# Four reorderings in a three-block transformer kernel: an output feature begun early, two copies moved, conversions cut in halves, a subtraction moved

## The reference

```
# block 1, sparse attention ("sparse stage")
score = sum_h relu(qi_h . ki) * w_h ; keep the 128 best keys of each token
p = softmax(q . k over the kept keys);  o = p @ c;  x += o @ a_w_out
# block 2, retention: 4 heads of 256, values of 512
s = (rotary(q) rotary(k)^T) * decay ; ret = s @ v
x += (rms_norm(ret) * silu(g)) @ b_w_out
# block 3, gated stage: three branches, each with a gate
y_a = (gelu u * spatial gating of v) @ w_a_out ; y_b = conv branch @ w_b_out
z = q k^T / 8 ; a = exp(log_sigmoid(z) + sum over later keys of log_sigmoid(-z))
y_c = (a @ v) @ w_c_out
x += (g0*y_a + g1*y_b + g2*y_c) @ w_out_2
```

## Time and profile before

| | us |
|---|---|
| median of three runs | 2094.62 |
| the profiled execution's own time | 2094.45 |
| its span, first to last instruction | 2092.7 |
| TensorE busy | 2077.5 (99%) |
| VectorE busy | 1461.1 (70%) |
| GpSimd busy | 1236.8 (59%) |
| ScalarE busy | 1145.1 (55%) |

### The profile page before, as it was taken

The page is one execution under the profiler, slowest core; times in us unless marked ns, Lnnn a source line. Parts: engine busy times, 40 slices in busy tenths (PEclk is TensorE's granted clock), DMA queues, the critical chain, the costliest instruction groups (busy, mean ns, idle before and its releaser), DMA issues.

```text
span 2092.7 us, 31674 instructions
## 1 busy us (share of the span) xinstructions
PE 2077.5 (99%) x11883; PEld 1819.7 (87%) x11883; DVE 1461.1 (70%) x2383; ACT 1145.1 (55%) x1892; POOL 1236.8 (59%) x763
## 2 busy tenths in 40 slices
PE   9999999999999999999999999999999999999999
PEld 7867889889899989988899898888887888899998
DVE  7973786767588777777776675997577325785773
ACT  6564654654554546456645544446777435645642
POOL 3514665874687778546658744655432554848843
PEclk9999999999999999999999999999999999999999
DMA  4203323333323232332333334322222242333232
GB/s 169 71 12 94 91 93 101 109 102 104 114 71 96 77 110 86 95 99 87 95 93 113 106 89 173 104 82 77 71 71 70 92 135 89 102 101 104 89 109 94
DMA packets 57687, 200.82 MB, mean 96 GB/s; under 512 B 6400, under 2 KB 7168, under 8 KB 57280
## 3 DMA queue, kind: packets, MB, share of 16 engines
q1 hardware_dynamic: 56816, 197.46, 29.9%
q10 hardware_dynamic: 720, 1.34, 0.2%
HBM read 194.32 MB, written 4.19 MB: 95 GB/s over the span
## 4 chain that ended last, share of the span: by engine, by line
PE 59%; DVE 1%; ACT 1%; issue 0%; ACTq 0%; DVEq 0%
PE ps L431 13%; PE ps L432 13%; PE ps L433 13%; PE ps L734 5%; PE ps L736 5%; PE ps L735 5%; PE ps L459 1%; PE ps L460 1%; PE ps L461 1%; PE ps L3005 1%; PE ps L2990 0%; PE ps L3017 0%; DVE ACC L632 0%; PE ps L2992 0%; PE ps L3014 0%
## 5 line engine op out<-in xcount | busy, mean ns | idle before, releaser
L409 POOL TENSOR_TENSOR WL<-WS,WH 128x1024 fp32r<-128x1024 f32 (+1 forms) x240 | 567.5, 2368 | 525.3 <-ACT WH L399 524.8
L431 PE MATMUL ps<-H,WH 128*128 128x512 f32 (+2 forms) x1264 | 492.9, 390 | 1.2 <-DVE H L639 0.7
L432 PE MATMUL ps<-H,WH 128*128 128x512 f32 (+2 forms) x1264 | 490.7, 388 | 0.0
L433 PE MATMUL ps<-H,WL 128*128 128x512 f32 (+2 forms) x1264 | 490.5, 388 | 0.0
L1246 POOL TENSOR_TENSOR WL<-WS,WH 128x512 fp32r<-128x512 f32 x232 | 312.3, 1359 | 226.5 <-ACT WH L857 224.6
L399 ACT ACTIVATE WH<-WS 128x1024 fp32r<-128x1024 f32 (+2 forms) x242 | 248.7, 1029 | 135.5 <-PE ps L433 66.6
L431 PEld LDWEIGHTS ps<-H,WH 128*128 128x128 f32 (+1 forms) x1264 | 237.0, 188 | 51.0 <-issue 2.7
L433 PEld LDWEIGHTS ps<-H,WL 128*128 128x128 f32 (+1 forms) x1264 | 236.9, 187 | 49.4
L432 PEld LDWEIGHTS ps<-H,WH 128*128 128x128 f32 (+1 forms) x1264 | 237.1, 188 | 46.3
L431 PE MATMUL ps<-G,WH 128*128 128x512 f32 x496 | 193.7, 391 | 2.2 <-DVE G L2724 1.4
L432 PE MATMUL ps<-G,WH 128*128 128x512 f32 x496 | 193.1, 389 | 0.0
(11 more groups left out here) (410 smaller groups left out, 4950.5 us busy)
## 6 DMA issues: line engine op xcount, KB each, us to landing
WS<-in_w SPq DMA_DIRECT2D x337, 512.0 KB, 3.5
WS<-in_w SPq DMA_DIRECT2D x24, 384.0 KB, 3.1
xs<-X SPq DMA_DIRECT2D x1, 2048.0 KB, 6.3
X<-xs SPq DMA_DIRECT2D x8, 256.0 KB, 3.7
out<-X SPq DMA_DIRECT2D x8, 256.0 KB, 2.0
X<-in_sg SPq DMA_DIRECT2D x1, 1344.0 KB, 5.6
X<-in_x ACTq DMA_DIRECT2D x4, 256.0 KB, 6.0
X<-in_x SPq DMA_DIRECT2D x4, 256.0 KB, 5.5
```

The source lines that it names most:

```text
L409: e.tensor_tensor(lo, raw, hi.bitcast(F), ALU.subtract).then_inc(*P.sig("w_lo", i))
L431: e.matmul(out, lh, rh, start=start, stop=False)
L432: e.matmul(out, lh, rl, start=False, stop=False)
L433: return e.matmul(out, ll, rh, start=False, stop=stop)
```

## The change

Four edits, none of which adds or removes arithmetic apart from the cut of three conversions.

1. Sparse stage: feature 2 is begun too (`D_OUT` has a third entry, 39, so its first half comes after the steps and ahead of TensorE's wait); features 3 to 7 remain whole. ScalarE makes unit 2's high part at its step 36.
2. Retention: in head 0, `u2` of the first gate pair goes ahead of two `decayed` copies and a form. In heads 0 to 2, `p5` of the k pair goes ahead of `y_high(h, 0)` and gets a wait for the row of head h.
3. Retention: the low part of `("bout", h, 0)`, h = 0 to 2, is made in two halves of 128x512, and TensorE waits for the first before z = 0 and for the second before z = 1.
4. Gated stage: VectorE adds the later keys' block (L3458) after the split of the item before (L3463), no longer ahead of it.

```diff
@@ lo_to
         e.wait_ge(*P.at("w_hi", i))
+        if in_halves(P.order[i]):
+            e.tensor_tensor(lo[:, 0:CELL], raw[:, 0:CELL], hi[:, 0:CELL].bitcast(F), ALU.subtract).then_inc(
+                *P.sig("k_sum", ("half", P.order[i])))
+            lo, raw, hi = lo[:, CELL:NXW], raw[:, CELL:NXW], hi[:, CELL:NXW]
         e.tensor_tensor(lo, raw, hi.bitcast(F), ALU.subtract).then_inc(*P.sig("w_lo", i))
+def in_halves(key):
+    return key[0] == "bout" and key[1] < 3 and key[2] == 0
@@ unit
         cells(P, key, 2)
+        if in_halves(key):
+            e.wait_ge(*P.at("k_sum", ("half", key)))
+        else:
+            e.wait_ge(*P.at("w_lo", P.index[key]))
+    elif in_halves(key):
         e.wait_ge(*P.at("w_lo", P.index[key]))
@@ act_ret, part
+        if name == "p5" and pair[0] == "qk" and pair[1] % 2:
+            e.wait_ge(*P.at("row", f"r{pair[1] // 2 - 1}"))
@@ act_ret
         part(one, "p5")
+        if h == 0:
+            part(one, "u2")
         decayed(h, 0)
         decayed(h, 1)
         forms(one, "a22")
-        part(one, "u2")
+        if h:
+            part(one, "u2")
...
             part(k, "p1")
+            part(k, "p5")
             y_high(h, 0)
-            part(k, "p5")
@@ sparse stage
-D_OUT = [36, 31]
+D_OUT = [36, 31, D_STEPS]
...
-    outs = [out_steps(m) for m in range(2)]
+    outs = [out_steps(m) for m in range(3)]
...
-    for m in range(2, 8):
+    for m in range(3, 8):
         feature(P, e, ("aout", m), outputs)
@@ act_dsa
         d_items(n, (4, cut), (0, logits), (6, values))
+        if n == D_OUT[0]:
+            hi_to(P, e, P.index.get(("aout", 2), 0) + 1)
@@ dve_gated, attend
             e.scalar_tensor_tensor(u, z, 0.0, u, ALU.max, ALU.add).then_inc(*P.sig("a_sp", k))
-            if kt < 3:
-                e.wait_ge(*P.at("a_sp", k))
-                e.tensor_tensor(u[:, 128:w], u[:, 128:w], c_soft(P, hd, kt + 1), ALU.add).then_inc(*P.sig("a_sp", (k, 1)))
         if it := c_stage(n, 2):
             ... (the split, L3463)
         if it := c_stage(n, 1):
             k, pr, kt, hd, w = it
+            u = c_soft(P, hd, kt)
+            if kt < 3:
+                e.wait_ge(*P.at("a_sp", k))
+                e.tensor_tensor(u[:, 128:w], u[:, 128:w], c_soft(P, hd, kt + 1), ALU.add).then_inc(*P.sig("a_sp", (k, 1)))
```

## The result

The changed kernel takes 2107.79 us (median of 5 runs, 2106.6 to 2108.92), the one before 2094.4 (5 runs, 2094.16 to 2095.47): the ratio is 1.0064, its interval 1.0049 to 1.0078. The profiled execution took 2108.55 with a span of 2106.7. The forecast of 2094.7 and its range (2091.0 to 2097.2) are missed, on the slow side, beyond even rival B's 2099.2.

A forecast was written before the change was run, and what follows sets the result against it. TensorE was taken as the bound, busy 2077.5 of 2092.7 us. Terms -0.5 - 0.75 - 0.6 - 1.35 + 3.3 = +0.1 us on the profiled 2094.45, 0.17 under the median 2094.62, gave 2094.7; range 2091.0 to 2097.2.

The forecast's parts named there:

- rival B: Gated stage: slipped ScalarE copies move conversions, so lone additions meet one; three meetings add 4.5 us, 2099.2; chance 0.06.
- Gated stage: Addition behind the split: low part late in eight of 24 items, +3.3 us, bounds -2.0 and +6.
- I worked out the same for all 24 additions: Gated stage, item by item: low part in time in 16, late in eight, 2.75 us plus 0.1 behind six new stalls.
- Item 14: Gated stage: conversions hold the addition and the low part, which comes 1.2 us after TensorE wants it.
- p5: Retention, heads 0 to 2: three a12 stalls go, most lost again at a22; 0.2 kept per head, -0.6 us.
- Rival A: Gated stage: low parts in time everywhere, both split stalls go; with other gains -6 us, 2088.5; chance 0.12.
- Sparse stage: Early feature 2 removes the stall at 159.61, -1.67 us; new wait at unit 3 costs 1.17; net -0.5 us.
- Retention: Three edits there: -0.75, -0.6 and -1.35 us.
- u2: Retention, head 0: the wait near 599 goes, copies behind slip 0.36 and their users come 3 us later; -0.75 us.
- the halves: Retention, three heads: output no longer waits for the whole low part; 0.43 stall and 0.05 behind go, -1.35 us.
- The signs listed beforehand: New profile: no waits near 599 and 638, a22 waits grown to about 0.4, no "issue" waits behind three k pairs.
- What would have made it wrong: Gated stage: forecast wrong if that stretch gets shorter or its waits pass 8 us; 4 to 6 us expected.

The follow-up runs named there:

- g_tinyconv: Kernel before with only the addition moved behind the split, and GpSimd's low parts of 24 gate and y units made over 8 of 1024 columns: 2097.79 us, ratio 1.0017.
- g_actorder: Kernel before with only the addition moved behind the split, and ScalarE's high copy behind the next item's abs, exp and ln: 2098.33 us, ratio 1.0015.
- b_halves: Kernel before with the low parts of the first two branches' gate and y units made in two halves: 2093.85 us, ratio 0.9997.
- rest: Changed kernel with the gated edit taken back, so the sparse and retention edits only, against the kernel before: 2093.29 us, ratio 0.9996.
- g_halves: Kernel before with only the addition moved behind the split, and the first two branches' gate and y low parts in two halves: 2101.74 us, ratio 1.0036.

## Why the prediction was wrong, step by step

**Gated stage, wrong, and the step that failed.** The step is "I worked out the same for all 24 additions", with the sum +3.3 us, where the stage grew by 15.2 by starts and the edit alone costs 12.6 at clock 1.000. It took every item with the starts of the kernel before: ScalarE's exponentials, the conversions and TensorE in their old places, and only the item's own chain lengthened. The chain's length was right: from the sums of item 30 to the end of item 31's low part the forecast had 4.7 us, and it took 4.58 in the changed kernel, by these rows, and 4.56 in g_tinyconv. (In the changed kernel TensorE is in a slow stretch there and reaches item 31's sums only at 1639.52, so this item, forecast 0.35 late, isn't.)

```profile
1633.58 0.75 PE L3038 MATMUL ps<-SC_cut,CX_cut 128*128 128x512 f32 x2 [1.92 <-DVE SC_cut L3492]
...
1637.47 0.69 DVE L3492 TENSOR_TENSOR SC_cut<-SC,SC_cut 128x512 fp32r<-128x512 f32 x1 [0.83 <-ACT SC_cut L3237]
...
1639.52 0.62 PE L3038 MATMUL ps<-SC_cut,CX_cut 128*128 128x512 f32 x2
```

Item 14 was not far off either, since it was priced with its conversions: 1.2 and 0.1 behind, against 1.78 by starts and a wait of 1.51:

```profile
1547.30 0.74 PE L3038 MATMUL ps<-SC_cut,CX_cut 128*128 128x512 f32 x2 [1.51 <-DVE SC_cut L3492]
```

What failed is that a late addition was taken to concern its own item alone. The high copy waits at the head of ScalarE's queue, with the logarithm of the next item, the exponentials, a weight copy and the gates' sigmoids behind it, so lateness that TensorE doesn't yet see is handed to the next item's split, and the next addition stands behind that. The measured chain of items 3 to 5 is this, and g_actorder bears it out by taking 10.2 of the 12.6 us back. It could have been seen: for p5 the prediction named what is queued behind the moved copy, and here it didn't.

The measured +15.2 by starts, by its largest parts: three 512-wide sums, +1.8, +1.3 and +2.0; five 384-wide ones, +1.4, +1.4, +1.0, +0.8 and +0.7; the bank, +2.2; two stretches at the lower clock, +3.2 in the profiled execution; and -1.8 for the two splits, which did go. That is 14.0; smaller steps make up the remainder. Of the eight sums the forecast had five: item 13 (0.25 forecast, 0.8 measured), item 14 (1.2 and 1.8), item 29 (0.2 and 1.4), and net of their splits item 15 (0.1 and 0.4) and item 30 (0.2 and 1.2). It had none of items 4, 5 and 20. The splits' going was forecast; the bank and the clock were not.

**The bank** is the same mechanism at its clearest. ScalarE, VectorE and TensorE in the profile after:

```profile
1585.35 1.63 DVE L3488 TENSOR_TENSOR SC<-SC 128x384 f32<-128x384 f32 x1
...
1587.08 0.63 ACT L3237 ACTIVATE SC_cut<-SC 128x512 fp32r<-128x512 f32 x1 [2.23 <-DVE SC L3488]
...
1588.91 1.28 ACT L3280 ACT_TABLE_LOAD   x1
...
1590.20 1.33 ACT L3280 ACTIVATE TMP<-TMP,PAR 128x512 f32<-128x512 f32 x2
1590.96 0.70 DVE L3539 TENSOR_TENSOR ps<-TMP,ps 128x512 f32<-128x512 f32 x1 [2.45 <-ACT TMP L3280]
...
1591.69 0.69 DVE L3541 TENSOR_TENSOR X<-X,ps 128x512 f32<-128x512 f32 x1
...
1592.43 0.50 PE L445 MATMUL ps<-H,WH 128*128 128x512 f32 x1 [1.93 <-DVE X L3541]
```

The addition meets a conversion (1.63 us), ScalarE idles 2.23 at the copy, and behind it the loading of ScalarE's function table (`ACT_TABLE_LOAD`) and the gate's sigmoids are late, then the two VectorE operations that free the bank. The release has nothing to do with the sums, to which my item-by-item sum was confined.

**Rival B**, at 0.06, had the right sign, stage and cause of spreading ("slips of ScalarE's copies"), and too small a price: 4.5 us for three meetings. Its argument against itself, that a conversion keeps its distance from the addition, failed: 13 additions are held by a GpSimd operation for over 0.7 us where 8 were. But the length of these meetings is not where the time went. The additions' busy sum didn't grow; what grew is who stands behind them. The Trainium skill, page "SBUF — State Buffer", section "Who interferes with whom", says that the side that issues second blocks fully for as long as the other instruction runs. The trace agrees (0.43 and 1.32 us for the same addition). By that rule alone one would count meetings, and g_tinyconv shows that 5.9 us come without the conversions.

**Rival A**: both splits went and gave -1.8 in the changed kernel. Without the gated edit they can be had: b_halves loses both.

**Sparse stage, right.** -0.5 forecast, -0.3 by starts, and the new wait is where the prediction had it: unit 3's low part ready at 170.05 and 1.07 us of waiting, against 170.20 and 1.05 measured.

**Retention, the signs of each mechanism right, the size wrong.** 2.7 us forecast; the three alone sum to -0.2 at clock 1.000, and rest keeps 0.8 by starts behind the sparse stage. For p5 the loss at a22 was foreseen and 0.2 a head kept; the trace keeps 0.0 to 0.1. For u2 ("their users come 3 us later") the user that mattered, the first copy of the next pair, was overlooked. For the halves it was the late low part of a unit 17 us later. The signs listed beforehand (the wait on L1837 at 0.4, no "issue" waits) all appeared; they tell that a wait went, and not that time was gained.

**What would have made it wrong**, "if its waits pass 8 us", is what happened: 10.5 us in the gated stage. (The eight terms of the gated sum add up to 2.74, not 2.75, which changes nothing.)

## What to carry to other kernels

When an edit makes an instruction wait, put on the bill everything that is queued behind the instructions waiting for it, engine by engine, until a slack of known size absorbs it; an item-by-item sum with all other engines held fixed gave 3.3 us here where the edit cost 12.6. A removed wait is worth the slack of the next event on each engine, and in this kernel, with TensorE busy 99%, each small wait of retention had one close behind it: price it alone, by the shift of later matmuls rather than by the wait's row. Before a subtraction is moved later, look whether the copy that waits for it can stand later in its queue, and price that by itself too, since here it cost 1.7 us.

## What the runs showed of the hardware that was not expected

**TensorE's clock falls for 3.4 us within a stretch in which it is busy 99%.** Nine matmuls of 512 columns instead of eighteen run in 3.40 us at a granted clock of 0.50, and 1.4 to 1.7 us are lost by starts (by runs 1.5 in the kernel before, 1.1 in the changed one, and nothing in g_halves). The falls in the gated stage stand behind waits of 1.9 us, and in g_halves at 1545.7, within a wait of 1.6 that ended at 1546.0. Nor do they come each time: by their mean clocks the five runs of the changed kernel hold two, one, one, two and none. One early in the sparse stage, behind a wait of 1.4 us for GpSimd, comes and goes between executions of kernels that are alike there: it is in the profile of g_tinyconv and not in that of the kernel before.

```profile
118.10:121.40 3.30, 3.17 (x7) 2.03 (x8) 1.37 (x6) 3.25 (x6) 0.33 (x1) 0.50 0.00 0
```

```profile
118.10:121.40 3.30, 3.21 (x11) 1.80 (x12) 1.40 (x6) 3.25 (x6) 0.30 (x1) 1.00 0.00 0
```

The kernel before has waits of up to 1.4 us once it is under way, and holds at least one such stretch in 6 of 27 to 12 of 33 runs, by series. The 1.51 us at 1547.30 of the changed kernel have no fall behind them. What decides whether a wait is followed by one is left open; no run was made for it. Such stretches are also why differences under 2 us are read here among runs at the same granted clock.
